# One attention unit for the first two query blocks, single accumulators for the modulations, and shifted work in two norms and the scan

## The reference, cut to what matters

```
mod = silu(c) @ w_ada + b_ada                # a vector of 6*1024, and for block 2 of 3*1024
h = rmsnorm(x) * (1 + sc1) + sh1
qa, ka, va, qb, ckv, qi, ki, wi = split(h @ w_in)
out_a = mixture of 3 dilated causal windows over qa, ka, va      (8 heads)
top = top_k(sum_h w[h] * relu(qi[h] . ki), 128 keys)             (indexer)
out_b = softmax(qb . keys(ckv) - slope*dist over top) @ values(ckv)   (8 heads)
x = x + ga1 * (concat(out_a, out_b) @ w_out)
x = x + ga2 * ((silu(gate) * up) @ w_down),  gate, up = rmsnorm(x)*(1+sc2)+sh2 @ w_gu
# second block
u = (rmsnorm(x)*(1+scale)+shift) @ w_in ; v = conv31(cv*sigmoid(cg))
y_conv = (silu(layernorm(v)) @ pw2) * silu(cs)
y_lru  = linear_scan(a, bx) * silu(ls),  a, bx from sigmoid gates of conv4(lx)
x = x + (1 + gate) * (concat(y_conv, y_lru) @ w_out) ; out = rmsnorm(x)
```

## Time and profile before

| | before |
|---|---|
| median of 3 runs | 1079.66 us (1077.78 to 1082.39) |
| profiled execution | 1078.11 us, its span 1076.3 us |
| TensorE busy | 1050.6 us, 98% of the span |
| VectorE, ScalarE, GpSimd busy | 57%, 38%, 41% |
| TensorE's granted clock, mean | 0.995 of full |

### The profile page before, as it was taken

The page is one execution under the profiler, slowest core; times in us unless marked ns, Lnnn a source line. Parts: engine busy times, 40 slices in busy tenths (PEclk is TensorE's granted clock), DMA queues, the critical chain, the costliest instruction groups (busy, mean ns, idle before and its releaser), DMA issues.

```text
span 1076.3 us, 14120 instructions
## 1 busy us (share of the span) xinstructions
PE 1050.6 (98%) x5290; PEld 848.2 (79%) x5290; DVE 618.2 (57%) x1222; ACT 409.2 (38%) x561; POOL 443.9 (41%) x155
## 2 busy tenths in 40 slices
PE   7999999999999999999999999999999999999997
PEld 5687786667878888888888888888887777787886
DVE  5357897675562332224346101579999998964322
ACT  4243325884241222212241222421226787362242
POOL 0034255392415353444433534335363555634350
PEclk9999999999999999999998999999999999999999
DMA  9983232040324435444373232223322222222312
GB/s 326 348 280 113 79 98 99 2 158 2 118 86 152 153 117 166 146 138 135 123 246 119 79 108 93 94 79 117 117 79 79 80 93 86 95 79 79 116 40 78
DMA packets 127251, 128.91 MB, mean 120 GB/s; under 512 B 3553, under 2 KB 125281, under 8 KB 127201
## 3 DMA queue, kind: packets, MB, share of 16 engines
q1 hardware_dynamic: 126240, 127.90, 36.6%
q10 hardware_dynamic: 960, 0.34, 0.1%
HBM read 126.13 MB, written 2.10 MB: 119 GB/s over the span
## 4 chain that ended last, share of the span: by engine, by line
PE 43%; issue 36%; POOL 14%; DVE 2%; SPq 1%; ACT 1%; DMA 1%; POOLq 0%; DVEq 0%; ACTq 0%
POOL w_lo L566 12%; PE bank L665 9%; PE bank L667 8%; PE bank L666 8%; PE bank L1009 2%; PE bank L982 2%; PE bank L1204 1%; PE bank L1205 1%; PE bank L1206 1%; PE bank L856 1%; DMA ada_stage<-in_w_ada 1%; POOL lru_lo L643 1%; PE bank L874 1%; PE bank L690 1%; PE bank L692 1%
## 5 line engine op out<-in xcount | busy, mean ns | idle before, releaser
L566 POOL TENSOR_TENSOR w_lo<-w_stage,w_hi 128x2048 fp32r<-128x2048 f32 x78 | 367.1, 4706 | 530.8 <-ACT w_hi L1275 530.8
L665 PE MATMUL bank<-act_hi,w_hi 128*128 128x512 f32 x848 | 335.8, 396 | 0.5 <-POOL w_lo L566 0.5
L667 PE MATMUL bank<-act_hi,w_lo 128*128 128x512 f32 x848 | 330.0, 389 | 0.0
L666 PE MATMUL bank<-act_lo,w_hi 128*128 128x512 f32 x848 | 330.0, 389 | 0.0
L1275 ACT ACTIVATE w_hi<-w_stage 128x2048 fp32r<-128x2048 f32 x78 | 149.3, 1914 | 255.9 <-PE bank L667 241.2
L665 PEld LDWEIGHTS bank<-act_hi,w_hi 128*128 128x128 f32 x848 | 159.3, 188 | 38.1 <-issue 6.3
L666 PEld LDWEIGHTS bank<-act_lo,w_hi 128*128 128x128 f32 x848 | 159.3, 188 | 33.8 <-issue 1.9
L667 PEld LDWEIGHTS bank<-act_hi,w_lo 128*128 128x128 f32 x848 | 159.2, 188 | 33.4
L2068 DVE SCALAR_TENSOR_TENSOR bank<-v_pad,vcol,bank 128x512 f32<-128x512 f32 x232 | 153.9, 748 | 0.0
L1984 DVE TENSOR_TENSOR tmp<-bank,tmp 128x512 f32<-128x512 f32 x22 | 15.2, 692 | 157.0 <-PE bank L667 153.6
L665 PE MATMUL bank<-ff_hi,w_hi 128*128 128x512 f32 x176 | 70.7, 402 | 0.0
(11 more groups left out here) (302 smaller groups left out, 1483.0 us busy)
## 6 DMA issues: line engine op xcount, KB each, us to landing
w_stage<-in_w_in SPq DMA_DIRECT2D x29, 1024.0 KB, 5.1
w_stage<-in_w_gu SPq DMA_DIRECT2D x22, 1024.0 KB, 5.2
ada_stage<-in_w_ada SPq DMA_DIRECT2D x20, 1024.0 KB, 11.7
w_stage<-in_w_out SPq DMA_DIRECT2D x12, 1024.0 KB, 5.2
ada_stage<-in_mod_w SPq DMA_DIRECT2D x12, 1024.0 KB, 7.9
w_stage<-in_w_down SPq DMA_DIRECT2D x8, 1024.0 KB, 5.2
late_stage<-in_w_ada SPq DMA_DIRECT2D x4, 1024.0 KB, 7.9
w_stage<-in_pw_w SPq DMA_DIRECT2D x4, 1024.0 KB, 5.1
```

The lines of the kernel that those rows point to most:

```text
L566: nc.gpsimd.tensor_tensor(w_lo[b][:], w_stage[b][:], w_hi[b][:].bitcast(F32), ALU.subtract).then_inc(s_lo, 1)
L665: pe.matmul(dst, wh, rhs_hi(k), start=(first and k == 0), stop=False)
L666: pe.matmul(dst, wh, rhs_lo(k), start=False, stop=False)
L667: mm = pe.matmul(dst, wl, rhs_hi(k), start=False, stop=(last and k == n_k - 1))
```

## The change

1. **Units.** Blocks 0 and 1 of a head pair become one unit (`SLOT_BLOCKS`), so there are 24 units, 3, 3 and 4 key blocks wide. Both blocks' scores share a bank. Its two score rows a head fill all four probs buffers, and an exponential waits for the turn of the unit that held its buffer four rows earlier. Of the second unit of a pair (block 2), ScalarE copies only the first head's turned blocks and VectorE the second's (`turned_second`, semaphore s_ptv). `spread_inverse`, the scaling and the split come a tick earlier. The last 12 top-k operations (one round and the six last ones) are issued two a tick from tick 2 on. `hi_part` of chunk C_OUT+1 moves from ahead of the attention to tick 2.
2. **Modulations.** `ada_step` keeps one accumulator and has a ninth step that adds the other half, so each product needs two matmuls in place of four. The five late products are spread over three tile ends (`LATE_AFTER`).
3. **Sums.** The norms' sums are taken with 128 columns of ones in place of one, and ScalarE reads the first column of each block.
4. **Start.** The second half of the first w_in chunk is loaded behind two more w_ada chunks.
5. **Scan and layer norm.** In the last of four steps GpSimd makes w_lo ahead of the gating products; ScalarE makes the gates ahead of `lru_high`; and the memset that releases the pw2 tiles stands before the layer norm's loop.

```diff
+SLOT_BLOCKS = ((0, 1), (2,), (3,))
+SLOTS = len(SLOT_BLOCKS)
+UNITS = [(g, j) for g in range(N_PAIRS) for j in range(SLOTS)]
+SPLIT = 1
+def blocks_of(v):
+    g, j = UNITS[v]
+    return [(i, n * (n + 1) // 2 if j == 0 else 0) for n, i in enumerate(SLOT_BLOCKS[j])]
+def width_of(v):
+    return sum(i + 1 for i, _ in blocks_of(v))
+def last_score(v):
+    g, j = UNITS[v]
+    return 2 * (TT * g + SLOT_BLOCKS[j][-1]) + 2
-ADA_ITEMS = KD
+ADA_ITEMS = KD + 1
+LATE_AFTER = {(0, 1, 1): (0, 1), (0, 2, 0): (2, 3), (0, 2, 1): (4,)}
-            for h in range(2):
+            def first_chunk_dma(h):
...
+            first_chunk_dma(0)
             w_in_dma(1)
-            for c in ADA_PE[2:]:
+            ada_dma(ADA_PE[2])
+            ada_dma(ADA_PE[3])
+            first_chunk_dma(1)
+            for c in ADA_PE[4:]:
                 ada_dma(c)
...
+                if p == KD // 2 - 1:
+                    lo(n, n % 2)
                 for k in (2 * p, 2 * p + 1):
                     pool.wait_ge(s_scan, k + 1)
...
-                        mm = pe.matmul(bank[b][:, t:t + 1], src[:, t * P:(t + 1) * P], ones[:, 0:1],
+                        mm = pe.matmul(bank[b][:, t * P:(t + 1) * P], src[:, t * P:(t + 1) * P], ones[:],
...
                 for m in range(2):
-                    for s in range(2):
-                        mm = pe.matmul(bank[7][:, 2 * c + m:2 * c + m + 1],
-                                       ada_acc[ADA_ACC[o]][:, s, m * P:(m + 1) * P], ones[:, 0:1], start=(s == 0), stop=(s == 1))
+                    mm = pe.matmul(bank[7][:, 2 * c + m:2 * c + m + 1],
+                                   ada_acc[ADA_ACC[o]][:, 0, m * P:(m + 1) * P], ones[:, 0:1], start=True, stop=True)
...
             def turn(v):
-                pe.wait_ge(s_exp, through(v))
+                pe.wait_ge(s_exp, last_score(v))
...
+                    if m == 1 and v >= 1 and UNITS[v - 1][1] == SPLIT:
+                        pe.wait_ge(s_ptv, UNITS[v - 1][0] + 1)
...
                 turn(tick + 1 - TURN_LAG)
+                for g in pair_at(tick, 1):
+                    spread_inverse(g)
...
-                    act.wait_ge(s_t, s - 3)
+                    g, i = divmod(s // 2 - 2, TT)
+                    act.wait_ge(s_t, 2 * (SLOTS * g + max(i - 1, 0)) + s % 2 + 1)
...
-            hi_part(C_OUT + 1, (C_OUT + 1) % 2, (C_OUT + 1) // 2)
...
+                if tick == 2:
+                    hi_part(C_OUT + 1, (C_OUT + 1) % 2, (C_OUT + 1) // 2)
...
+                if t == KD:
+                    dve.wait_ge(s_adastep, steps[0])
+                    V.tensor_tensor(acc[:, 0, :], acc[:, 0, :], part, ALU.add).then_inc(s_adaacc, 1)
+                    return
...
+            def turned_second(v):
+                n = width_of(v)
+                dve.wait_ge(s_t, through(v))
+                if v >= 3:
+                    dve.wait_ge(s_pv, through(v - 3))
+                V.tensor_copy(pairT[v % 3][:, 1, 0:n, :].rearrange("p k q -> p (k q)"),
+                              bank[TURN_BANK[1]][:, 0:P * n]).then_inc(s_ptv, 1)
...
+                if tick >= 2:
+                    top_steps(2)
                 for g in pair_at(tick, 1):
                     invert_sums(g)
-                for g in pair_at(tick, 3):
+                for g in pair_at(tick, 2):
                     copy_spread(g)
-                for g in pair_at(tick, 4):
+                for g in pair_at(tick, 3):
                     scale_pair(g)
+                if SPLIT <= tick - 1 < N_U and UNITS[tick - 1][1] == SPLIT:
+                    turned_second(tick - 1)
...
             inverse()
+            V.memset(nothing[:, 2:3], 0.0).then_inc(s_yc, 4)
             dve.wait_ge(s_spread, 5)
...
-            V.memset(nothing[:, 2:3], 0.0).then_inc(s_yc, 4)
```

More of the change, by code:

```diff
@@ L200, in build @@
         ada_bufs.append(ada1)
-        ada_acc = [fixed(f"ada_acc{b}", [P, 2, NCOL])[0] for b in range(2)]
+        ada_acc, at_acc = map(list, zip(*[fixed(f"ada_acc{b}", [P, 2, NCOL]) for b in range(2)]))
         qaT, at_qa = fixed("qaT", [P, 4, T])
@@ L1129, in _ @@
                             mm.then_inc(s_racc, 1)
-                if m2 == 0:
-                    for b in range(len(ADA_LATE)):
-                        late_products(b)
+                        for b in LATE_AFTER.get((m2, g, m), ()):
+                            late_products(b)
             square_sums(gained=True)
@@ L1468, in _ @@
                 if tick < N_U:
-                    for m in range(2):
-                        exponentials(2 * tick + m, P * (UNITS[tick][1] + 1))
+                    unit_exponentials(tick)
                 if tick == 2:
@@ new lines, in least_of @@
+                for i, at in blocks_of(v):
+                    n = P * (i + 1)
+                    for m in range(2):
+                        s, h = 2 * (TT * g + i) + m, 2 * g + m
+                        scores = bank[SCORE_BANK[v % 2][m]][:, at * P:at * P + n]
+                        dve.wait_ge(s_s, last_score(v) - 1 + m)
+                        if v < N_A:
+                            dve.wait_ge(s_tab, h + 1)
+                            least(s, scores, table[h % 4][:, T - n:T])
+                        else:
+                            dve.wait_ge(s_comb, s - N_FIRST + 1)
+                            least(s, scores, comb[s % 4][:, 0:n])
@@ new lines, in _, with top_steps @@
+            dve.wait_ge(s_score, 2 * len(PAIRS))
+            top = [0]
+            def top_steps(count):
+                for _ in range(min(count, TOP_STEPS - top[0])):
+                    at = top[0] - 3
+                    top[0] += 1
+                    if at < 0:
+                        i = at + 4
+                        d = score[i][:, i * P:(i + 1) * P]
+                        V.tensor_tensor(d, d, causal[:, 1, :], ALU.min).then_inc(s_top, 1)
+                        continue
+                    r, step = divmod(at, 6)
+                    i = step % 3 + 1
+                    src = (score if r == 0 else work)[i][:]
+                    dve.wait_ge(s_top, at + 1)
+                    if r == TOPK // 8 and step < 3:
+                        V.tensor_tensor(work[i][:], work[i][:], score[i][:], ALU.is_equal).then_inc(s_top, 1)
+                    elif r == TOPK // 8:
+                        V.tensor_scalar(work[i][:], work[i][:], BIG, None, ALU.mult).then_inc(s_top, 1)
+                    elif step < 3:
+                        V.max(top8[i][:], src).then_inc(s_top, 1)
+                    else:
+                        V.match_replace(work[i][:], top8[i][:], src, -3.0e38).then_inc(s_top, 1)
```

159 lines of the change are left out of this document (70 added, 89 removed).

## The result

The changed kernel took 1073.04 us (median of 5 runs, 1072.65 to 1073.72) against 1079.03 for the kernel before (5 runs, 1077.78 to 1082.39). The ratio of the changed kernel to the one before is 0.9942, with a 95% interval of 0.9928 to 0.9955. It is 6 us faster; I had forecast 15, with a range of 1059 to 1070. Profile against profile the span went from 1076.3 to 1071.8, 4.5 us. The time saved was there until 911 us in the program; most of it was gone 28 us later. Of the three signs of being wrong that I had named, two showed: the total is above 1072, and a low clock stands near 930 us. The third, the mean's products without a wait, did not.

A forecast was written before the change was run, and what follows sets the result against it. The prediction took the kernel as one long TensorE stream, busy 98% of the span. Its terms summed to -15.1 us, taking the median of 1079.66 to 1064.6; it forecast 1064.5, range 1059 to 1070.

The forecast's parts named there:

- three signs of being wrong: Total above 1072 us, a low clock anywhere between 20 and 1065 us, or the mean's products coming without a wait.
- The modulations: 12 modulation chunks in the tile streams: four instructions instead of eight, 0.36 us instead of 0.81 each, -5.4 us.
- the load order: At the start, half a w_in chunk loads later, so TensorE waits less for the fourth w_ada chunk: -1.5 us.
- (a): Five late products at 0.36 us each plus two more tile restarts: 2.0 us instead of 5.91, -3.9 us.
- (b): Nine matmuls behind the late products take 2.06 us instead of 3.82 if the clock doesn't fall: -1.8 us.
- the memset: TensorE's wait for the memset, behind the mean, goes away: -0.9 us.
- The 128 columns: Norm sums with 128 columns, 11 calls of four products: +0.3 us in all, bounds 0 and +1.5.
- term (c): 387 matmuls behind the clock dip ran 0.0044 us slower each; if that hangs on the dip, -1.7 us.
- the clock: At the late products, spreading the one-column stretch keeps the clock up; rival, the dip stays: +3.5, 1068 us, chance 0.18.
- scan and layer norm: Waits for w_lo (1.5) and gates (1.2) go but become a wait at the mean: -0.2 us, bounds 0 and -2.7.
- five of my cases: Forecast's own case 0.54; dip stays 1068, 0.18; attention pays 1069.5, 0.13; more gained 1059, 0.09; clock falls in attention 1089, 0.02.
- the attention: Head pairs: fewer piece starts (-2.0) against tighter waits and the head; sum +0.6, taken as 0, bounds -5 and +5.

The follow-up runs named there:

- u_ada2: a_units32_wlo with two accumulators per modulation chunk again, eight instructions in place of four, late products still spread: 1071.04 us.
- u_scan0: a_units32_wlo with ScalarE's gates behind lru_high and the memset behind the layer norm's loop, as before the change: 1064.54 us.
- b_att: The kernel before with the new attention of 24 units alone, its head included: 1083.59 us, ratio 1.0034.
- b_wlo: The kernel before with only w_lo moved ahead of the gating products in the last scan step: 1089.90 us, ratio 1.0093.
- b_late: The kernel before with the five late products spread over three tile ends, still eight instructions each: 1077.77 us, ratio 0.9973.
- u_late1: a_units32_wlo with the five late products, four instructions each, all at the place of the last one: 1065.17 us.
- u_sums1: a_units32_wlo with the norms' sums taken with one column of ones, as before the change: 1065.68 us.
- a_units32: The changed kernel with the attention as before (32 units, top-k's last operations and hi_part where they stood): 1070.41 us.
- a_hi_top: The changed kernel, still 24 units, with hi_part and the last six top-k operations placed as before: 1071.22 us.
- a_wlo: The changed kernel with w_lo behind the gating products again in the last scan step: 1067.07 us, ratio to before 0.989.
- a_units32_wlo: The changed kernel with the old attention of 32 units and w_lo behind the gating products again: 1064.18 us, ratio to before 0.9854.
- a_hi_top_wlo: The changed kernel, still 24 units, with hi_part, the last six top-k operations and w_lo placed as before: 1064.79 us.

## Where the prediction was right and wrong

**Right: the terms on TensorE alone.** The modulations (forecast -5.4 for the 12 in the streams; 0.36 against 0.81 in the rows, and 6.9 us with the late ones in u_ada2), the load order (-1.5; -1.44), the late products (the terms (a) and (b), -3.9 and -1.8; -3.7 and -1.7) and the memset (-0.9; -0.98 in the profiles, 0.4 or less in the medians of u_scan0) came near what I set. The 128 columns cost what I booked where the clock is up (+0.3 for all; +0.09 for a norm).

**Right by luck: term (c), -1.7.** From 302 to 680 us the changed kernel gains 7.07 against my 7.4, and 1.7 of it is the quicker cadence, which I hung on the dip. b_att and b_wlo have the dip and the quick cadence, so the dip is not its cause. The slow cadence belongs to the one profile of the kernel before that I had read; why it ran so is open.

**Right at its place, too narrow as a reading: the clock.** TensorE was never idle around the fall at the late products, and spreading the products (b_late) or halving them (u_late1) keeps the clock up there, while all three profiles with the 40 instructions together (before, b_att, b_wlo) have the fall. But I treated it as one place's affair and the quick norm sums of the earlier trace rows as proof that they are safe. b_late, b_att and b_wlo, all of them the kernel before in their first 79 us, show low clock at 31 us (behind the wait for w_ada) and at 79 (behind two modulation products in a row, 16 instructions of one column), where the profile of before has none, and all three have it in the norm behind w_down. So the same instructions run with or without it. Three parts of the change take such places away at once: the halved products (u_ada2, which doubles them again, has low clock at 76), the load order, and the 128 columns, which I booked as a cost of 0.3 and without which u_sums1 is 1.5 us slower, 1.1 of it at a norm in its profile. It would also explain why the medians differ by 6.0 us and these two profiles by 4.5. The runs of the kernel before point the same way: the mean granted clock was 0.994 in the run of 1077.61 us and 0.985 in that of 1083.00. The stretches of low clock in each profile, the end of the program left out:

| kernel | low clock at (us) |
|---|---|
| before | 584.6 to 591.4 |
| changed | 929.3 to 939.5 |
| a_units32, a_hi_top | 925.5 to 936; 928 to 935 |
| a_wlo, a_units32_wlo, u_scan0 | none |
| a_hi_top_wlo, u_late1 | 912.5 to 916.5; 910 to 914 |
| u_sums1 | 295.5 to 299.5, 913.5 to 917.5 |
| u_ada2 | 76 to 80 |
| b_late | 31 to 34.5, 78.5 to 82.5, 683 to 690 |
| b_att | 30.5 to 34.5, 78.5 to 82.5, 590.5 to 597.5, 689.5 to 693 |
| b_wlo | 31 to 35, 79 to 83, 587.5 to 595, 686.5 to 690.5, 946 to 956.5 |

**Wrong: "scan and layer norm", -0.2 with bounds of 0 and -2.7.** This is the step that failed the forecast, with 6 us in the medians and 8.1 in the profiles (a_wlo against the changed kernel). Its premise was right: VectorE's sum and TensorE meet at the mean with nothing to spare, so earlier products on TensorE give nothing. I then forecast a wait of 2 to 3 us and said that VectorE's steps "don't get shorter". I never asked whether they could get longer. The moved w_lo is a GpSimd instruction of 4.6 us on SBUF operands, and the place to which it moved is the one where VectorE multiplies and scans SBUF tiles. I priced what it takes from TensorE's wait and left out what it does to its neighbour. What the runs showed in its place: VectorE held 5.5 us (4.1 and 1.4), a wait of 8.2 on TensorE where I had 2 to 3, and 2.4 more of low clock. The rows ahead of the run could have priced the first hold: w_lo's 4.6 us against VectorE's 1.28, so up to 4.6 us on a chain with no slack. The Trainium skill's rule on the ports, above, names the case. All five of my cases left it out, and the bound of 0 was no bound.

**Wrong in size: the attention, 0 with bounds of -5 and +5.** It cost 2.6 us (a_units32) and 3.0 in the profiles, inside the bounds. Of its parts, the starts of pieces that I took as -2.0 are nearly nothing: two pairs hold 16.50 us of busy TensorE in the changed kernel, against 2 x 8.32 = 16.64. The idle time in the pairs came as I set it (0.66 us a pair; I had 0.5 to 0.7). The head's wait of up to 1.5 for vb came as 1.63. The top-k operations, of which I said only that they "may add to it", cost the largest wait, 1.84. The head together, by a_hi_top, is 1.8 of the 2.6, and 2.4 of 2.9 in the profiles.

**Right: gains upstream pass VectorE.** The lead of 10.8 us at the end of w_down appeared on VectorE too (11.3 us at 886.36), since its convolution starts on what TensorE gives it. What the gates take away on ScalarE's side is worth 0.2 us at the first lru product (u_scan0), as forecast.

Sum with what was measured: without the moved w_lo and with the old attention the remaining parts give 1064.18, close to the forecast's 1064.5; the two parts that it had at -0.2 and 0 cost 6.0 and 2.6 to 2.9. That the rest comes out so close is partly luck, as term (c) had no cause in the change and the 128 columns gained where I had booked a cost.

## What to carry to other kernels

When a step moves on GpSimd, lay its new interval over VectorE's rows: an instruction there that reads two SBUF tiles (here a product, a scan and an addition) can be held to its end, and that is a price on VectorE's chain even where GpSimd itself has room. Where two engines meet with no slack, ask of the one that isn't sped up whether the change can slow it, and remember that a long wait on TensorE is paid again in clock: all four profiles with the wait of 8.2 us have low clock behind it. Before hanging a slow stretch on an event in one profile, look at a second profile that has the event. Undo the parts of a bundled change one at a time before keeping it: here two pieces cost 9 us out of a possible 16.

## What the runs showed of the hardware

TensorE's clock can fall to 1.2 GHz while TensorE is busy the whole time with one-column or narrow products: 584.6 to 591.4 with 6.80 us busy of 6.80, and in b_late 682.5 to 689.5 with 7.00 of 7.00. Whether a given narrow stretch does it differs from run to run of the same instructions, which is probably part of why the runs of the kernel before range from 1077.45 to 1083.00 while the four of a_units32_wlo stay within 1.1 us. Products of a float32 block with 128 columns cost what those with one column cost (3.65 against 3.56 us for the same sums) and none of the nine profiles with 128 columns has low clock at a norm. Behind the fall at the late products the following 387 matmuls ran 0.0044 us slower each at full granted clock in the kernel before. They didn't in any other profile, not in b_att and b_wlo either, which have the same fall; why is open. A VectorE instruction on two SBUF tiles that starts behind a GpSimd instruction on SBUF tiles waits for its end (4.74, 2.12, 5.57 and 2.90 us in place of 0.64, 0.70, 1.20 and 0.70), and GpSimd is held by VectorE in the same way (6.15 in place of 4.6); VectorE's steps with one operand in PSUM kept their 0.66 us.
